# Two transformer blocks on one core: 64-column projections computed once and copied across partitions

## What is computed

```
first block, per layer:  qa 512, ka 512, va 512, qi 512, ki 64, wi 8, cq 384, ckv 256, kr 32, gates 2048
second block:            aq 512, ak 512, av 512, bq 512, kc 128, vc 128, ksl 128, vsl 128, kw 128, vw 128, gl 24
```

## Time and profile before

| | |
|---|---|
| median of 3 runs | 2604.97 us (2601.32 to 2613.48) |
| profiled execution, device time | 2607.02 us |
| its span, first to last instruction | 2605.2 us |
| PE busy | 2495.5 us (96%) |
| POOL busy | 1851.3 us (71%) |
| DVE busy | 1254.5 us (48%) |
| ACT busy | 612.1 us (23%) |
| chain that ended last | PE 74%, POOL 15%, rest 11% |
| mean granted PE clock | 0.972 |

### The profile page before, as it was taken

How to read it: one execution, slowest core, us unless ns; L and a number is a source line. 1 busy time by engine, 2 the same in 40 slices (tenths; PEclk the granted TensorE clock), 3 DMA queues, 4 the chain that set the end, 5 groups by cost and what they waited for, 6 DMA issues and landing times.

```text
span 2605.2 us, 35786 instructions
## 1 busy us (share of the span) xinstructions
PE 2495.5 (96%) x11509; PEld 1835.8 (70%) x11509; DVE 1254.5 (48%) x2207; ACT 612.1 (23%) x1403; POOL 1851.3 (71%) x856
## 2 busy tenths in 40 slices
PE   7999999999999999999999999999989999999997
PEld 4665577777777766656777777777876557777776
DVE  5565654475326347666445651464312663641352
ACT  3232620221001223245004110113001663100001
POOL 5663368878888875633888888888587226888885
PEclk9998999999999999999999999999699789999999
DMA  5222013222222222210222222323523001233322
GB/s 179 73 66 89 18 57 94 93 81 89 90 96 89 89 82 65 73 66 18 89 91 90 87 89 91 91 86 105 169 89 114 1 2 61 89 94 94 92 89 80
DMA packets 62454, 214.70 MB, mean 82 GB/s; under 512 B 6440, under 2 KB 6696, under 8 KB 62320
## 3 DMA queue, kind: packets, MB, share of 16 engines
q1 hardware_dynamic: 54432, 195.90, 23.9%
q10 hardware_dynamic: 7888, 17.06, 2.2%
HBM read 210.78 MB, written 10.01 MB: 85 GB/s over the span
## 4 chain that ended last, share of the span: by engine, by line
PE 74%; POOL 15%; issue 3%; ACT 3%; DVE 3%; DVEq 2%; DMA 0%; ACTq 0%; POOLq 0%; PEldq 0%
PE out_tile L457 62%; POOL w_lo L1671 8%; POOL w_hi L1665 7%; PE turned L601 3%; PE stat L615 2%; PE out_tile L883 1%; PE turned L578 1%; ACT sq L1015 1%; PE out_tile L752 1%; PE out_tile L757 1%; DVEq L1292 1%; PE out_tile L669 1%; ACT arena L1025 1%; PE out_tile L762 1%; PE out_tile L772 0%
## 5 line engine op out<-in xcount | busy, mean ns | idle before, releaser
L457 PE MATMUL out_tile<-arena_r,w_hi 128*128 128x512 f32 (+1 forms) x5418 | 1710.8, 397 | 0.0
L457 PEld LDWEIGHTS out_tile<-arena_r,w_hi 128*128 128x128 f32 x5418 | 1028.0, 190 | 233.4 <-issue 2.2
L1665 POOL TENSOR_TENSOR w_hi<-weight_ring,cst 128x1024 fp32r<-128x1024 f32 x359 | 877.8, 2445 | 437.3 <-PE out_tile L457 418.7
L457 PE MATMUL out_tile<-arena_r,w_lo 128*128 128x512 f32 (+1 forms) x2709 | 1101.6, 407 | 40.9 <-POOL w_lo L1671 24.4
L1671 POOL TENSOR_TENSOR w_lo<-weight_ring,w_hi 128x1024 fp32r<-128x1024 f32 x359 | 887.2, 2471 | 27.8
L457 PEld LDWEIGHTS out_tile<-arena_r,w_lo 128*128 128x128 f32 x2709 | 515.2, 190 | 258.8 <-POOL w_lo L1671 88.1
L1270 DVE TENSOR_TENSOR x<-out_tile,x 128x512 f32<-128x512 f32 x72 | 49.8, 692 | 345.4 <-PE out_tile L457 345.3
L1207 DVE CAST arena_r<-work 128x512 f32 (+2 forms) x84 | 189.1, 2251 | 13.2 <-issue 11.9
L1133 ACT ACTIVATE work<-out_tile,p 128x512 f32<-128x512 f32 x88 | 66.0, 775 | 394.0 <-PE out_tile L457 306.5
L1532 DVE SCALAR_TENSOR_TENSOR work<-out_tile,p,work 128x511 f32<-128x511 f32 x88 | 65.7, 746 | 179.1 <-ACT work L1133 179.1
L1689 POOL TENSOR_SCALAR work<-work,small 128x128 f32<-128x128 f32 (+2 forms) x60 | 35.2, 587 | 149.3 <-DVE small L1324 149.3
(11 more groups left out here) (179 smaller groups left out, 1907.1 us busy)
## 6 DMA issues: line engine op xcount, KB each, us to landing
weight_ring<-stream SPq DMA_DIRECT2D x364, 512.0 KB, 3.5
arena<-bias_rows ACTq DMA_DIRECT2D x4, 2048.0 KB, 10.1
bias_rows<-bias_kept ACTq DMA_DIRECT2D x3, 2556.0 KB, 16.0
x<-x_t SPq DMA_DIRECT2D x4, 512.0 KB, 9.3
out_t<-arena SPq DMA_DIRECT2D x8, 256.0 KB, 2.2
cst<-consts SPq DMA_DIRECT2D x1, 576.0 KB, 14.2
arena<-spread ACTq DMA_DIRECT2D x1, 256.0 KB, 8.8
cst<-consts SPq DMA_DIRECT2D x1, 244.0 KB, 8.5
```

Source lines behind the costliest of these rows:

```text
L457: ins = pe.matmul(out, l, r, start=start and n == 0, stop=stop and n == 2, **kw)
L1665: pool.tensor_tensor(w_hi[:, s % SPLIT, :].rearrange("p (w c) -> p w c", c=P), ring[:, s, :].rearrange("p (w c) -> p w c", c=P), ones.unsq ...
```

## The change

1. `ki` is no projection of its own. Its 64 columns lie in the free columns of `misc`; ACT takes `misc` in two copies of 64 partitions (`wi` and `kr` to `misc`, the key to the upper half of `ki`), DVE copies the upper half to the lower (`index_keys`), and PE waits for that ahead of `cq`. One more pad tile and one more empty result keep the counts.
2. `kc`, `vc`, `ksl` and `kw` are one projection of 128 columns each, 8 blocks in place of 16, all four ahead of `hk`. DVE copies each half to both halves of a buffer (`both_halves`: four copies of 64x512 from PSUM). The reordering by 16 tokens (`split_blocks`) then reads `kc` and `vc` from SBUF (`work`) and no longer from PSUM. `hk` and `hv` wait for `blocks_ready`.
3. `v2` comes directly after `hv`, and `kcmp` and `vcmp` after `v2`.
4. POOL splits only 280 of each 512 columns of the `v2` tiles. A table `used`, one entry a tile, says how much; an entry `two` is meant for the tile that holds the two blocks of `kcmp` and `vcmp` and six of padding.
5. The stream is 360 tiles long.

```diff
-W1_BLOCKS = dict(qi=32, misc=8, ki=8, cq=24, ckv=16, qa=32, uqr=6, uqn=12, kn=8, fill=6, ka=32, va=32, vb=8, pad=16, merge=192,
+W1_BLOCKS = dict(qi=32, misc=8, cq=24, ckv=16, qa=32, uqr=6, uqn=12, kn=8, fill=6, ka=32, va=32, vb=8, pad=24, merge=192,
...
-W2_BLOCKS = dict(aq0=16, kc=16, vc=16, w1=32, w2=2, padw=6, ksl=16, kw=16, v2=32, aq=16, ak=32, av=32, bq=32, out=64,
+W2_BLOCKS = dict(aq0=16, kc=8, vc=8, ksl=8, kw=8, w1=32, v2=32, w2=2, padw=6, aq=16, ak=32, av=32, bq=32, out=64,
...
-                linear(("misc",), h_mix, DC, m=96)
-                linear(("ki",), h_mix, DC)
+                linear(("misc",), h_mix, DC)
...
                 A.wait_taken(pe, L, ("qi", 1))
-                A.wait_taken(pe, L, ("ki",))
+                pe.wait_ge(index_keys, L + 1)
...
-            linear_pair((("kc", 0), ("kc", 1)), h_mix, DC, ready=LAYERS * 5 * DC + DC)
-            for g in range(2):
-                linear(("vc", g), h_mix, DC)
+            linear_pair((("kc",), ("vc",)), h_mix, DC, ready=LAYERS * 5 * DC + DC)
+            for name in ("ksl", "kw"):
+                linear((name,), h_mix, DC)
...
-                B.wait_taken(pe, 0, last)
+                pe.wait_ge(blocks_ready, n + 1)
...
                 ins.then_inc(B.tile_done, 1)
+            token_major("v2", h_mix, DC, V2)
             w2k, w2v = weight(), weight()
...
             weight(wide=W2_BLOCKS["padw"])
-            for name in ("ksl", "kw"):
-                for g in range(2):
-                    linear((name, g), h_mix, DC)
-
-            token_major("v2", h_mix, DC, 2 * P + 24)
...
-                take_tile(("misc",), misc[0:96, 0, :], 96)
-                take_tile(("ki",), ki[:, 0, :])
+                A.wait_done(act, L, ("misc",))
+                both = psum[A.tile_no(("misc",)) % 4]
+                act.activation(misc[0:HD, 0, :], both[0:HD, :], ACT.Copy)
+                act.activation(ki[HD:P, 0, :], both[HD:P, :], ACT.Copy).then_inc(A.taken["a"], 1)
...
+                A.wait_taken(dve, L, ("misc",))
+                plain(dve)
+                dve.tensor_copy(ki[0:HD, 0, :], ki[HD:P, 0, :]).then_inc(index_keys, 1)
...
+            def both_halves(name, dst):
+
+                ps = tile(B, 0, (name,))
+                for g, half in enumerate((lower, upper)):
+                    for to in (lower, upper):
+                        ins = dve.tensor_copy(dst(g)[to], ps[half, :])
+                took(ins, B)
...
-                    src = ps[:, :].rearrange("p (n r) -> p r n", r=16)
+                    tokens = src(g).rearrange("p (n r) -> p r n", r=16)
...
+            both_halves("kc", lambda g: work[:, g, :])
+            both_halves("vc", lambda g: work[:, 2 + g, :])
+            dve.drain()
+            split_blocks(kc, lambda g: work[:, g, :])
+            both_halves("ksl", lambda g: ksl[:, g, :])
+            both_halves("kw", lambda g: kw[:, g, :])
+            split_blocks(vc, lambda g: work[:, 2 + g, :])
...
+            whole, values, two = (WT, P), (WT // 4, V2), (2, P)
...
+            at, used = 0, {}
+            for k, blocks in W2_BLOCKS.items():
+                for n in range(at // WT, (at + blocks) // WT if k != "w2" else at // WT + 1):
+                    used[first + n] = values if k == "v2" else two if k == "w2" else whole
+                at += blocks
+            for n in range(first, ready):
+                split_tile(n, n % RING, 16 * (n // RING + 1), used[n])
```

More of the change, by code:

```diff
@@ L116 @@
 SPREAD_AT = {k: n for n, k in enumerate(SPREADS)}
+NONE = 3
+V2 = 2 * P + 24
 def index_batch(n):
@@ L123, in plan_first @@
 def plan_first():
-    t = [(("qi", c), "v" if c < 2 else "a") for c in range(4)] + [(("misc",), "a"), (("ki",), "a"), (("wi",), "v")]
+    t = [(("qi", c), "v" if c < 2 else "a") for c in range(4)] + [(("misc",), "a"), (("wi",), "v")]
     for n, key in enumerate(BESIDE_INDEX):
@@ L131, in plan_first @@
     t += [(("va", b), "a") for b in range(QB)] + [(("vb", b), "a") for b in range(QB)]
-    t += [(("none", n), "a") for n in range(2)]
+    t += [(("none", n), "a") for n in range(NONE)]
     t += attention_tiles(ITEMS_1)
@@ L680, in _ @@
                     for i in range(4):
-                        ins = pe.matmul(ps[32 * i:32 * i + 32, :], lhs[64:96, 64:96], misc[64:96, 0, :], start=True,
+                        ins = pe.matmul(ps[32 * i:32 * i + 32, :], lhs[32:64, 32:64], misc[32:64, 0, :], start=True,
                                         stop=True)
@@ L734, in pads_over @@
                         pe.nop().then_inc(weights_begun, 1)
-                    for _ in range(2):
+                    for _ in range(NONE):
                         pe.nop().then_inc(A.tile_done, 1)
@@ L1100, in _ @@
                     take_tile(("vb", b), vb[:, b, :])
-                A.wait_done(act, L, ("none", 1))
+                A.wait_done(act, L, ("none", NONE - 1))
                 A.wait_taken(act, L, ("vb", QB - 1))
                 plain(act)
-                for _ in range(2):
+                for _ in range(NONE):
                     act.sem_inc(A.taken["a"], 1)
@@ L1557, in _, with split_blocks @@
                     dve.memset(part.bitcast(F32), 0.0)
-            for name, buf in (("kc", kc), ("vc", vc)):
+            lower, upper = slice(0, HD), slice(HD, P)
+            def both_halves(name, dst):
[4 more added lines that the diff above has]
+                took(ins, B)
+            def split_blocks(buf, src):
                 for g in range(2):
-                    ps = tile(B, 0, (name, g))
                     places = []
@@ L1594, in _ @@
                 split(t, gelu(e, slice(0, 64))).then_inc(gelu_done, 1)
-            for name, buf in (("ksl", ksl), ("kw", kw)):
-                for g in range(2):
-                    took(dve.tensor_copy(buf[:, g, :], tile(B, 0, (name, g))[:, :]), B)
             for b in range(QB):
@@ L1658, in _, with blocks_of, split_upper @@
         def _(pool):
-            def split_upper(number, s, arrived, begun=None):
+            whole, values, two = (WT, P), (WT // 4, V2), (2, P)
+            def blocks_of(tile, used):
+                n, width = used
+                space = WT * P // n if used == values else P
+                return tile.rearrange("p (w c) -> p w c", c=space)[:, 0:n, 0:width]
+            def split_upper(number, s, arrived, begun=None, used=whole):
                 pool.wait_ge(landed[s], arrived)
@@ L1690, in normalise @@
                                    ALU.mult).then_inc(sec.prob_even, 1)
-            before = -(-sum(W1_BLOCKS[k] for k in ("qi", "misc", "ki", "cq", "ckv", "qa", "ka", "va", "uqr", "uqn", "kn", "fill", "vb")) // WT)
+            before = -(-sum(W1_BLOCKS[k] for k in ("qi", "misc", "cq", "ckv", "qa", "ka", "va", "uqr", "uqn", "kn", "fill", "vb")) // WT)
             pads = W1_BLOCKS["pad"] // WT
@@ L1711, in _ @@
                     split_tile(*place(n))
+                pool.wait_ge(weights_split, L * W1_TILES + before)
                 for n in range(before, go_on):
@@ L1730, in _ @@
             first, last = LAYERS * W1_TILES, LAYERS * W1_TILES + W2_TILES - W2_BLOCKS["pad"] // WT
-            ready = first + sum(W2_BLOCKS[k] for k in ("aq0", "kc", "vc", "w1", "w2", "padw", "ksl", "kw", "v2", "aq", "ak", "av",
+            ready = first + sum(W2_BLOCKS[k] for k in ("aq0", "kc", "vc", "ksl", "kw", "w1", "v2", "w2", "padw", "aq", "ak", "av",
                                                        "bq")) // WT + 1
-            with pool.Fori(first // RING, ready // RING) as i:
-                group(i * RING, i)
-            for n in range(ready // RING * RING, ready):
-                split_tile(n, n % RING, 16 * (n // RING + 1))
+            at, used = 0, {}
[5 more added lines that the diff above has]
+                split_tile(n, n % RING, 16 * (n // RING + 1), used[n])
             for n in range(0, B.turns, 2):
```

48 lines of the change are left out of this document (25 added, 23 removed).

## The result

The changed kernel takes **2537.9 us**, the median of four runs (2537.0 to 2538.9), where the kernel before takes 2606.3 (four runs, 2601.3 to 2613.5): a ratio of 0.974, 95% interval 0.971 to 0.976. I had forecast 2575 us, range 2562 to 2590. The sign was right; the saving was 68 us where I expected some 30.

What follows compares the result with a forecast made beforehand. PE was taken as the bound in long projections. The rebuilt stretch took 93.9 us against 116.0, saving 22, with the layers 30.4: 2607.0 became 2576.6, forecast as 2575 because the profiled run lay 2.0 above the median; range 2562 to 2590.

Steps and rivals of the forecast that it cites:

- the first one: Long stretches of full projections: PE is the bound at 5.7 us a tile and POOL keeps up.
- `ki` in `misc`: Both layers, from `misc` to `cq`: folding the key in saves 4.2 us a layer, 8.4 us in all.
- the clock behind the pause: Rival, 10%: low clock lasts through `v2` and follows the longer pauses behind `misc` (2 x 1.7 us); 2583 us.
- Mask, pads, empty results: Mask clearing moved into `va`, third pad during `vb`: hidden by other work, counted at nothing.
- `kc`, `vc`, `ksl`, `kw` in 22.84 us: Second block: four tiles stand where `kc` and `vc` had four, 22.84 us again; the later 25.09 us disappear.
- Wait of `hk`: PE ahead of `hk` waits 5 us for DVE's new work; bounds 3.2 and 12.2 us.
- Eight copies: DVE ahead of `hk`: copies of 64x512 from PSUM at 0.6 us each, 4.8 us together.
- The twelve steps: DVE ahead of `hk`: four long casts, four long subtractions, four short steps from SBUF; upper bound 18.7 us.
- `hk` and `hv` 41.0 us at the low level: Second block: their 192 matmuls run at the low clock from the start, 41.0 us; bounds 38.3 and 41.0.
- wait of `hv`: PE ahead of `hv`: DVE has all of `hk` for its work, so 0 us; upper bound 3 us.
- `v2`: Directly behind `hv`: first tile 5.6 us, two tiles 6.8, second products after 5.5, wait for `aq` 5.5; 23.4 us.
- The clock behind the pause ahead of `aq`: Start of the rest of `aq`: the clock is low after the pause, costing 1.7 us; bounds 0 and 2.3.

## Why the prediction was off

The step that failed is the first one: *"In the long stretches of full projections PE is therefore the bound and POOL keeps up"*. I tested it on the four tiles of `kc` and `vc`, where DVE works from PSUM, and carried it to the 196 tiles of the layers' merge, output and feed-forward, where it often does not. Two signs stood in what I had read. POOL's idle time of 437 us, "nearly all of it for PE", is 1.2 us a tile, and 0.74 of that is a hand-over, not slack. And POOL had 15% of the chain that ended last, which I put in a table and did not ask about. By that step a shorter split could only be worth nothing, and I did not list the edit to its operand as a part of the change, so it stands in the sum at nothing. The runs showed 42.0 us by its removal and 45.8 alone, because POOL's cycle with its hand-over, 5.64 us, was as long as PE's 5.62 and DVE lengthened it to 5.91 in the layers' feed-forward.

The other steps, against the changed kernel and the runs:

- `ki` in `misc`: forecast 4.2 us a layer; alone 2.8 and 3.0. The steps were right (1.98 us for 2.30, DVE's copy 0.42 for 0.69), the clock behind the pause was left to a rival and happened.
- Mask, pads, empty results at nothing: nothing seen.
- `kc`, `vc`, `ksl`, `kw` in 22.84 us: 22.95.
- Wait of `hk` 5 us: 5.00, with luck in it. Eight copies took 5.65 us, not 4.8: 1.40 us for 1023 columns is 0.70 for 512, not the 0.6 that I read. The twelve steps took 10.7 us, where my 5 us implies 11.5, and the two errors cancel. The choice near the lower bound held because POOL stood still; where projections stood ahead of `hk`, the steps took 13.7 and 17.4 us.
- `hk` and `hv` 41.0 us at the low level: 40.95. No wait of `hv`: none; DVE was done 3.6 us ahead.
- `v2`: from its start to the second products 16.67 us, forecast 5.6 + 6.8 + 5.5 = 17.9; the cycle was 3.2 us for 3.4. The tile of the second products at its full width cost a wait of 1.61 us, and 3.73 us followed behind; forecast 5.5 us for the step, measured 4.93. Both forecasts carried POOL's old 4.8 us for a full tile, where it took 4.3.
- The clock behind the pause ahead of `aq` was low, as forecast: 0.61 over the first 5 us.
- The range of 2562 to 2590 took in bounds for each term that I had, and none for a term that I did not. With the operand put back the kernel takes 2579.9 us, inside it, and the second block's projection stage saves 22.2 us, where I had 22.

## What to carry to other kernels

Before calling an engine hidden, add up its whole cycle, hand-over included, and set it beside the bound engine's: 5.64 against 5.62 us is no room, and what lengthens its work (here DVE's steps with SBUF inputs in the layers) is then paid in full in each cycle. Read a diff by instructions and operands, not by its theme: one changed operand in the innermost helper outweighed four restructured stages. And steps that run free in another engine's pause may slow down when that pause is filled.

## What the chip showed that I had not expected

- POOL, 1024 columns of float32 per partition: product with a 128-column block repeated 2.40 us, with one repeated column 1.89, copy 1.04; the subtraction of two full inputs 2.40.
- DVE's casts and subtractions from SBUF with a step of 16 words, left alone by POOL: three casts of 512, 480 and 31 columns 1.65 us, three subtractions 2.09, against 1.40 and 1.46 from PSUM. That is 1.6 and 2.0 ns a column (1023 columns); a cast of 128x512 without a step takes 0.43 us undisturbed, 0.8 ns a column. The Trainium skill (Vector Engine (DVE) Microarchitecture Reference, Measured stream behaviour on trn2) has 2.5 ns a column where both sources, or the destination alone, step by 24 words. Here, with one source stepped by 16, it was less, and `hk` waited 5.00 us and not the 7 that I had estimated from the page.
- Short matmuls (64 and 2 columns), block by block among full ones, ran at 2.4 GHz throughout; in runs of eight blocks they did not; alone they ran at 1.2 GHz for 41 us. The mixing halved their price without a change to them: a mixed tile of 5.49 us less four full blocks at 0.70 leaves 0.67 us for six, where they took 1.28.
